# A state-space scan beside a projection: units of two pairs, sums on GpSimd, and an earlier first unit

## The reference, cut to what matters

```python
def s5_mix(u, a_re, a_im, b_re, b_im, c_re, c_im, d, log_step, w_glu, b_glu):
    uf = u.reshape(B, L, S5_GROUPS, S5_GROUP)             # 32 groups of 16 channels
    abar_re, abar_im = mag * cos(ang), mag * sin(ang)
    bu_re = einsum('blgc,gnc->blgn', uf, bbar_re)          # 64 states per group
    bu_im = einsum('blgc,gnc->blgn', uf, bbar_im)
    _, _, s_re, s_im = associative_scan(_complex_affine_combine, elems, axis=1)
    y = (einsum('blgn,gcn->blgc', s_re, c_re) - einsum('blgn,gcn->blgc', s_im, c_im)
         + d * uf)
    y = gelu(y.reshape(B, L, MIX_W))
    return y * sigmoid(y @ w_glu + b_glu)

# in second_block:
h = rms_norm_2(x, norm_mix[l])
p_rw, p_s5, p_gla, p_gate = split(h @ w_in[l])             # u of S5 is p_s5: 512 of the columns
```

## Time and profile before

| | us |
|---|---|
| median of 3 runs | 2916.47 (2916.03 to 2916.61) |
| the profiled execution | 2917.33 |
| its span, first to last instruction | 2916.0 |
| TensorE busy | 2858.7, 98% |
| VectorE busy | 1619.2, 56% |
| ScalarE busy | 652.4, 22% |
| GpSimd busy | 5.0, 0% |

### The profile page before, as it was taken

The page is one execution under the profiler, slowest core; times in us unless marked ns, Lnnn a source line. Parts: engine busy times, 40 slices in busy tenths (PEclk is TensorE's granted clock), DMA queues, the critical chain, the costliest instruction groups (busy, mean ns, idle before and its releaser), DMA issues.

```text
span 2916.0 us, 36187 instructions
## 1 busy us (share of the span) xinstructions
PE 2858.7 (98%) x14760; PEld 1961.6 (67%) x14760; DVE 1619.2 (56%) x3196; ACT 652.4 (22%) x1347; POOL 5.0 (0%) x22
## 2 busy tenths in 40 slices
PE   8999999999999999999998999999999999999998
PEld 3567588888544575888885445455554875688886
DVE  5675544453336855466746984455452633666654
ACT  5651300000136513100000021422220102222200
POOL 0000000000000000000000000000000000000000
PEclk9999999999999999999999999999999999999999
DMA  4013122222211231222221111211112331222222
GB/s 146 29 51 101 51 94 87 87 99 97 80 60 49 73 109 66 94 73 87 88 100 65 51 58 58 72 45 45 45 45 93 110 108 46 78 90 89 88 87 80
DMA packets 61941, 224.25 MB, mean 77 GB/s; under 512 B 6992, under 2 KB 7248, under 8 KB 61264
## 3 DMA queue, kind: packets, MB, share of 16 engines
q1 hardware_dynamic: 61776, 221.94, 22.7%
HBM read 219.82 MB, written 2.10 MB: 76 GB/s over the span
## 4 chain that ended last, share of the span: by engine, by line
PE 93%; DVE 6%; issue 1%; ACT 0%; DMA 0%; SPq 0%; DVEq 0%; ACTq 0%
PE ps L1636 29%; PE ps L647 18%; PE ps L1059 15%; PE ps L1047 8%; PE ps L1112 4%; PE ps L1418 3%; PE ps L1391 2%; PE ps L1074 2%; PE ps L1403 2%; PE ps L2796 1%; PE ps L2102 1%; PE ps L2123 1%; PE ps L2319 1%; PE ps L2966 1%; PE ps L1717 1%
## 5 line engine op out<-in xcount | busy, mean ns | idle before, releaser
L1059 PE MATMUL ps<-h,ring 128*128 128x512 f32 x784 | 362.5, 606 | 0.0
L1636 PE MATMUL ps<-h,ring 128*128 128x256 f32 x1136 | 270.7, 381 | 8.5 <-DVE u L1658 4.6
L1059 PEld LDWEIGHTS ps<-h,ring 128*128 128x128 f32 x784 | 143.1, 191 | 159.5 <-issue 153.5
L1636 PEld LDWEIGHTS ps<-h,ring 128*128 128x128 f32 x1136 | 215.9, 191 | 44.0 <-issue 8.7
L1636 PE MATMUL ps<-h_sums,w_sums 128*128 128x256 f32 x1008 | 224.4, 379 | 0.0
L1636 PEld LDWEIGHTS ps<-h_sums,w_sums 128*128 128x128 f32 x1008 | 191.5, 190 | 26.0
L647 PE MATMUL ps<-hid_sums,d_sums 128*128 128x256 f32 x720 | 171.2, 379 | 1.0 <-DVE hid_sums L1595 1.0
L647 PEld LDWEIGHTS ps<-hid_sums,d_sums 128*128 128x128 f32 x720 | 136.6, 190 | 20.3 <-issue 1.8
L1577 DVE TENSOR_TENSOR d_sums<-ring 128x512 f32<-128x512 f32 (+1 forms) x48 | 31.5, 656 | 172.0 <-DMA ring<-stream_dram 172.0
L1112 PE MATMUL ps<-o_x,ring 128*128 128x512 f32 x256 | 112.2, 593 | 0.0
L1636 PE MATMUL ps<-c_h_sums,c_sums 128*128 128x256 f32 x504 | 112.2, 379 | 0.0
(11 more groups left out here) (613 smaller groups left out, 4739.3 us busy)
## 6 DMA issues: line engine op xcount, KB each, us to landing
ring<-stream_dram SPq DMA_DIRECT2D x395, 512.0 KB, 3.7
bias<-bias_dram SPq DMA_DIRECT2D x8, 448.0 KB, 4.3
mem<-mem_dram SPq DMA_DIRECT2D x3, 1024.0 KB, 5.0
x<-x_dram SPq DMA_DIRECT2D x4, 512.0 KB, 7.5
out_dram<-x SPq DMA_DIRECT2D x8, 256.0 KB, 2.2
rope_ab<-ropes_dram SPq DMA_DIRECT2D x4, 256.0 KB, 8.6
s_big<-s_big_dram SPq DMA_DIRECT2D x1, 1024.0 KB, 6.9
constants<-constants_dram SPq DMA_DIRECT2D x1, 768.0 KB, 11.5
```

The costliest lines, as they stand in the source:

```text
L1059: mm = pe.matmul(out, w, r, start=(k == 0), stop=(k == len(rhs) - 1))
L1636: mm = pe.matmul(ps[:, bank + at, 0:256], w(k), x(k), start=start and k == 0, stop=k == 3, skip_group_check=not start)
```

## The change

Four things change together.

- *Units.* TensorE now makes `inputs` and `outputs` for units of two pairs, four state tiles: `inputs(n)` is eight products into banks 0 to 3, `outputs(n)` sixteen into bank 4 or 5. A unit thus takes all four banks, so `inputs(n + 1)` waits until VectorE has read both pairs of unit n. The 16 pairs of VectorE's loop stay.
- *Sums.* The two sums of a pair leave VectorE for GpSimd. `s5_m` becomes two buffers, and VectorE multiplies pair q + 1 (`turned_inputs`) ahead of the scans of pair q.
- *u.* All four tiles of u now come from the unscaled h: column u2 goes to bank 6, u3 to bank 5, and VectorE multiplies both by root behind its first pair.
- *Order.* TensorE issues `inputs(0)` in the middle of column u2; VectorE does its first pair before it scales h. 104 side steps remain (nine columns and `gla_v`): 14 ahead of the first outputs, then 2 and 11 around `inputs(n + 1)`.

```diff
@@ TensorE
+                def inputs(n):
+                    a, i = divmod(n, 4)
+                    if n:
+                        pe.wait_ge(*s['s5_mod'].at(8 * n))
+                    if a == 0:
+                        pe.wait_ge(*s['s5_u'].at(i + 1))
                     for j in range(2):
-                        for e in range(2):
+                        for e in range(4):
...
+                def outputs(n):
+                    i = n % 4
+                    pe.wait_ge(*s['s5_dem'].at(2 * n + 2))
+                    if n:
+                        pe.wait_ge(*(s['s5_y'].at(n - 1) if n > 1 else s['s5_u'].at(4)))
...
                 self.contract(pe, ps[:, 7, :], h, s['projected'])
+                third = self.contract_steps(pe, ps[:, 6, :], h, s['projected'], False)
+                for _ in range(4):
+                    next(third)
+                inputs(0)
+                for _ in third:
+                    pass
+                self.contract(pe, ps[:, 5, :], h, s['projected'])
                 side = columns()
-                inputs(0)
-                inputs(1)
-                for q in range(16):
-                    for _ in range(8):
+                for n in range(8):
+                    for _ in range(2 if n else 0):
                         next(side, None)
-                    outputs(q)
-                    if q + 2 < 16:
-                        inputs(q + 2)
+                    if n < 7:
+                        inputs(n + 1)
+                    for _ in range(11 if n else 14):
+                        next(side, None)
+                    outputs(n)
@@ VectorE
-                for k in range(DT):
-                    dve.tensor_tensor(h[k], h[k], self.root[:, :], ALU.mult).then_inc(*s['prepared'].up())
                 dve.tensor_scalar(cneg[:, :], t.big[:, 2, :], -1.0, None, ALU.mult).then_inc(*s['vec'].up())
+                def turned_inputs(q):
+                    mq, g, b = m[q % 2], 2 * pairs[q][1], 2 * (q % 2)
+                    er, ei = t.er[:, g:g + 2, :], t.ei[:, g:g + 2, :]
+                    dve.wait_ge(*s['s5_in'].at(q // 2 + 1))
+                    re, im = ps[:, b:b + 2, 0:half], ps[:, b:b + 2, half:2 * half]
+                    for j, (x, y) in enumerate(((re, er), (im, ei), (im, er), (re, ei))):
+                        dve.tensor_tensor(mq[:, j, :, :], x, y, ALU.mult).then_inc(*s['s5_mod'].up())
+
+                dve.wait_ge(*s['vec'].now())
+                turned_inputs(0)
                 for q, (a, p) in enumerate(pairs):
...
                     dve.wait_ge(*s['vec'].now())
-                    dve.tensor_tensor(m[:, 3, :, :], re, ei, ALU.mult).then_inc(*s['s5_mod'].up())
-                    dve.tensor_tensor(m[:, 0, :, :], m[:, 0, :, :], m[:, 1, :, :], ALU.add).then_inc(*s['vec'].up())
-                    dve.wait_ge(*s['s5_mod'].at(q + 1))
-                    dve.tensor_tensor(m[:, 2, :, :], m[:, 2, :, :], m[:, 3, :, :], ALU.subtract).then_inc(*s['vec'].up())
-                    dve.wait_ge(*s['vec'].now())
+                    if q < 15:
+                        turned_inputs(q + 1)
+                    dve.wait_ge(*s['s5_add'].at(2 * q + 2))
...
                     if q >= 2:
-                        dve.wait_ge(*s['s5_out'].at(q - 1))
+                        dve.wait_ge(*s['s5_out'].at(q // 2))
...
+                    if q == 0:
+                        for i, bank in ((2, 6), (3, 5)):
+                            dve.wait_ge(*s['projected'].at(i + 1))
+                            dve.tensor_tensor(u[:, i, :], ps[:, bank, :], self.root[:, :], ALU.mult).then_inc(*s['s5_u'].up())
+                        for k in range(DT):
+                            dve.tensor_tensor(h[k], h[k], self.root[:, :], ALU.mult).then_inc(*s['prepared'].up())
@@ GpSimd
+            @block.gpsimd
+            def _(pool):
+                for q in range(16):
+                    mq = m[q % 2]
+                    pool.wait_ge(*s['s5_mod'].at(4 * q + 4))
+                    pool.tensor_tensor(mq[:, 0, :, :], mq[:, 0, :, :], mq[:, 1, :, :], ALU.add).then_inc(*s['s5_add'].up())
+                    pool.tensor_tensor(mq[:, 2, :, :], mq[:, 2, :, :], mq[:, 3, :, :], ALU.subtract).then_inc(*s['s5_add'].up())
```

More of the change, by code:

```diff
@@ L2763, in columns @@
                 def columns():
[L2764 to L2778, removed]
+                    for i in range(4, len(dense)):
+                        pe.wait_ge(*(s['freed'].at(i - 5) if i >= 6 else s['s5_u'].at((3, 2)[i - 4])))
+                        yield from self.contract_steps(pe, ps[:, 6 + i % 2, :], h, s['projected'], i == 4)
@@ L2779, in inputs @@
+                    yield from self.token_steps(pe, [6, 7], h, s['projected'], s['freed'], len(dense) - 4)
+                def inputs(n):
[4 more added lines that the diff above has]
+                        pe.wait_ge(*s['s5_u'].at(i + 1))
                     for j in range(2):
-                        for e in range(2):
-                            r, i = rows(2 * p + e), p // 2
-                            mm = pe.matmul(ps[:, 2 * (q % 2) + e, half * j:half * (j + 1)], t.bt[r, j, i * P:(i + 1) * P],
-                                           u[r, i, half * a:half * (a + 1)], start=True, stop=True)
+                        for e in range(4):
+                            mm = pe.matmul(ps[:, e, half * j:half * (j + 1)], t.bt[rows(e), j, i * P:(i + 1) * P],
+                                           u[rows(e), i, half * a:half * (a + 1)], start=True, stop=True)
@@ L2784, in inputs @@
                     mm.then_inc(*s['s5_in'].up())
[L2786 to L2792, removed]
+                def outputs(n):
[3 more added lines that the diff above has]
+                        pe.wait_ge(*(s['s5_y'].at(n - 1) if n > 1 else s['s5_u'].at(4)))
+                    c = lambda e: slice(32 * (4 * i + e), 32 * (4 * i + e) + 32)
@@ L2793, in outputs @@
                     for j in range(4):
-                        for e in range(2):
+                        for e in range(4):
                             w = (t.big[:, 2, c(e)], cneg[:, c(e)], t.big[:, 3, c(e)], t.big[:, 3, c(e)])[j]
-                            mm = pe.matmul(ps[rows(2 * p + e), 4 + i % 2, 0:half], w, o[:, q % 2, j, e, :],
+                            mm = pe.matmul(ps[rows(e), 4 + i % 2, 0:half], w, o[:, e // 2, j, e % 2, :],
                                            start=(j == 0), stop=(j == 3))
@@ L2806, in _ @@
                 self.contract(pe, ps[:, 7, :], h, s['projected'])
+                third = self.contract_steps(pe, ps[:, 6, :], h, s['projected'], False)
[5 more added lines that the diff above has]
+                self.contract(pe, ps[:, 5, :], h, s['projected'])
                 side = columns()
-                inputs(0)
-                inputs(1)
-                for q in range(16):
-                    for _ in range(8):
+                for n in range(8):
+                    for _ in range(2 if n else 0):
                         next(side, None)
-                    outputs(q)
-                    if q + 2 < 16:
-                        inputs(q + 2)
+                    if n < 7:
[3 more added lines that the diff above has]
+                    outputs(n)
                 for _ in side:
                     pass
-            self.s5_end, self.y_read = s['s5_out'].at(16), [s['s5_y'].at(7), s['s5_y'].at(8)]
-            self.v_read = [s['freed'].at(len(dense) + k) for k in (1, 2)]
+            self.s5_end, self.y_read = s['s5_out'].at(8), [s['s5_y'].at(7), s['s5_y'].at(8)]
+            self.v_read = [s['freed'].at(len(dense) - 2 + k) for k in (1, 2)]
             @block.scalar
@@ L2835, in _ @@
                 for i, out in enumerate(dense):
-                    if i < 2:
+                    if i < 4:
                         continue
@@ L2902, in _ @@
                             first = t.init[:, j, g + e:g + e + 1] if a else 0.0
-                            dve.tensor_tensor_scan(z[:, j, e, :], mag, m[:, 2 * j, e, :], first, ALU.mult,
+                            dve.tensor_tensor_scan(z[:, j, e, :], mag, m[q % 2][:, 2 * j, e, :], first, ALU.mult,
                                                    ALU.add).then_inc(*s['vec'].up())
                     if q >= 2:
-                        dve.wait_ge(*s['s5_out'].at(q - 1))
+                        dve.wait_ge(*s['s5_out'].at(q // 2))
                     dve.wait_ge(*s['vec'].now())
@@ L2927, in s5_skip @@
         t = slice(256 * a, 256 * (a + 1))
[L2928 removed]
+        dve.wait_ge(*self.s['s5_out'].at(k + 1))
         dve.scalar_tensor_tensor(out=y[:, i, t], in0=u[:, i, t], scalar=self.v('s5_d', i), in1=self.ps[:, 4 + i % 2, 0:256],
@@ L3338, in second_block @@
         gd, v, u = p('gla_gd', [P, S], 32), p('gla_v', [P, 4, S], 34), p('u_s5', [P, 4, S], 42)
-        self.s5_inputs(down, both, square, self.s5_tables, u, y_s5, qk, go, gd, v, p('s5_m', [P, 4, 2, 256], 50), p('s5_z', [P, 2, 2, 256], 58),
```

(1 more changed line is left out.)

8 lines of the change are left out of this document (1 added, 7 removed).

## The result

| | us | runs |
|---|---|---|
| before, median | 2916.05 (2914.26 to 2917.56) | 20 |
| after, median | 2920.51 (2919.15 to 2922.0) | 20 |
| ratio, 95% interval | 1.0016 (1.001 to 1.0021) | |
| after, profiled execution | 2921.03, span 2919.3 | 1 |

The forecast was 2916, so no change. The kernel became slower by 4.5 us. That is less than the 0.2% I had called a difference, but all 20 runs of after are above all 20 of before.

The account below looks back on a forecast made before the run. TensorE bounds the kernel before (9.97 us a pair against VectorE's 8.79), VectorE the changed one. From 2917.3, minus 28 for structure, plus 27 for stalls by GpSimd's sums, gives 2916.3, said as 2916 us; range 2889 to 2928.

Parts of the forecast that it names:

- TensorE's side: TensorE in the loop: four tiles run at once, unit outputs 1.85 and inputs 1.06 us; some 35 us leave.
- both gaps: TensorE's idle times at the loop's start, 2.79 us for u0 and 4.76 us for pair 0, predicted to go.
- VectorE becomes the bound: In the loop, VectorE needs 15.4 us a unit against TensorE's 14.5; 28 us gained if GpSimd's sums cost VectorE nothing.
- The whole, at the middle of the two prices, 0.90 us: VectorE's scans and turned products stand still for each whole GpSimd sum: 30 x 0.90 = 27 us.
- The break-even of 0.93: The cost to VectorE of one GpSimd sum, 0.93 us, at which the change neither gains nor loses.
- The slow clock, 4.5 us: TensorE's half-clock stretch after its 4.76 us idle time at the loop's start, predicted to go, saving 4.5 us.
- The rest at nothing: Behind the loop's last outputs both kernels go on alike, so everything there was costed at nothing.
- The cover for TensorE's waits: TensorE idles some 5 us a unit; 7.9 us of its work at slow clock hides behind VectorE's 9.1 us.
- Free: GpSimd's sums and VectorE don't disturb each other, or sums run only beside products out of PSUM: 2889 us; chance 0.26.
- Half: One sum of each pair fits VectorE's wait between scans and turned products, its second beside products: 13.5 us, 2903; chance 0.16.
- Blocked and dear: Same stall of VectorE, but a GpSimd sum above 1.1 us: slower by over 0.2%, 2929 us at 1.35; chance 0.24.
- Not what it says: TensorE's order might not pack four tiles; with VectorE stalled by sums, some 3 us more, 2919; no chance given.

Follow-up runs that it names:

- Experiments 2 to 5: Changed kernel with sums held until VectorE reads PSUM, 2898.08 us; memsets replacing sums, 2888.85; kernel before plus extra GpSimd sums, 2940.61; changed kernel with copies replacing sums, 2899.89.
- experiments 10 and 11: The changed kernel and the kernel before, each run once more unchanged: 2920.55 us and 2916.32 us.

## Why the prediction was wrong

1. **TensorE's side: right.** Unit outputs 1.86 and inputs 1.07, so four tiles run at once; both gaps are gone.
2. **VectorE becomes the bound: right.** So are the lengths without sums: with memsets the phase is shorter by 28.6 us, where the text has 28. That is measured against the first profiled execution of before.
3. **"The whole, at the middle of the two prices, 0.90 us": the step that failed, by its size.** That VectorE stands still, in which instructions, and that pair 0 escapes is as I wrote. The price is 1.02 us in the first half and 0.96 in the second (from the means of 32 scans each, 1181 less 672 ns for 16 sums and 1151 less 732 ns for 14). Over all thirty the phase gives 30.1 / 30 = 1.00, so the term is 30.1 and not 27, and the phase comes out 1.5 us longer instead of 1 us shorter. A pair takes VectorE 9.60 and 9.85 us in turn in the first half, where I had 9.3 to 9.5. The break-even of 0.93 lay 0.03 above my choice, so a price known only to lie between 0.45 and 1.35 decided the sign, and I took the middle. The Trainium skill, "GPSIMD Engine Reference", section "Elementwise — side-by-side cycle accounting", has 4497 ns for 2048 columns, an estimate of 1.12 us a sum; the measured 1.22, beside products out of PSUM, is nearer to that than to my 0.90. The Trainium skill, "SBUF — State Buffer", section "Who interferes with whom", says that an instruction of VectorE with two SBUF inputs excludes one of GpSimd that reads SBUF, and one with a single SBUF input does not. Experiments 2 to 5 agree: 1.02 us lost to a sum and 0.36 to a copy beside scans, nothing to a memset, and nothing beside products out of PSUM.
4. **The slow clock, 4.5 us: mis-sized as well.** I counted it as a property of the kernel. In a second execution the same gap cost 1.7. Against the mean of the two profiles of before the structure gains about 27 us and not 28.6; this is why the phase differs by 1.5 us in the two first profiles and by 2.9 over all four.
5. **The rest at nothing: wrong, 2.2 us in the first profiles of the two kernels.** Of these 1.2 lie ahead of the phase, in a longer stretch at half clock that comes with and without the change (experiments 10 and 11); 0.6 behind it, which over all four profiles are under 0.1; and 0.4 outside the span, in every execution of after, with its cause open. With this the forecast's sum closes: 2916.3 + 3.1 (sums) - 0.6 (structure) + 2.2 = 2921.0 us, the profiled execution of after. With the right price alone it would have been 2919.4, 2 us above before and still what I called no change.
6. **The cover for TensorE's waits: right.** 4.88 us before the outputs, the clock down to 0.83 in some stretches, VectorE busy all the same.
7. **The rivals.** *Free* is what the structure would have given; memsets reach it to the microsecond. *Half* is excluded. *Blocked and dear* began at 1.1 us a sum; the measured price lies below, and the 4.5 us stay under its 0.2%. *Not what it says* did not occur.

## What to carry to other kernels

Work moved to GpSimd was not taken off VectorE here as long as VectorE read two operands from SBUF: a sum worth 0.6 to 0.7 us there cost it 1.02. Before moving such work, find the stretch in which VectorE reads PSUM and hold GpSimd back until then; one wait was worth 22 us. And when a forecast's sign hangs on one price that no row shows, say that the sign is open, and compare with more than one execution where a slow-clock stretch is part of the sum, or lies anywhere ahead of the phase.

## What the runs showed of the hardware

- A GpSimd sum of 128x512 takes 1.22 us beside VectorE's products out of PSUM and 1.55 to 1.65 beside its scans; a copy 0.56 and 0.9; a memset 0.52.
- VectorE's loss to them beside scans is 1.02, 0.36 and 0 us, for sum and copy the shorter length less 0.20. It appears as duration of the instruction, so busy shares hide it.
- A VectorE operation of 16 columns, 0.17 us, takes 1.27 when a sum is in its way.
- VectorE's products out of PSUM keep their 0.68 us beside a sum.
- The stretch at half clock after nearly the same TensorE gap lasted about 10 us in one execution and about 3.5 in another; one at 1304 us, in code that did not change, 3.4 or 6.8.
